# Building the new x from its normed form, and splitting the last ten expert matrices: one change to a decoder block with 32 experts

## The reference

```
h = rms_norm(x, g_mix);  z = h @ w_in + b_in          # w_in 1024 x 5376
y_conv = silu(layer_norm(conv31(glu))) @ w_conv_out + b    # 31 taps per channel
y_attn = window_attention(q, k, v, sinks) @ w_attn_out + b # window 128, 16 heads
x = x + (gate_conv * y_conv + gate_attn * y_attn) @ w_out
x = x + moe(rms_norm(x, g_ffn))     # 32 experts, top 4 per token, softmax weights
return rms_norm(x, g_final)
# one expert: a = (clip(u)+1) * g*sigmoid(1.702 g), g = min(x@w_gate+b, 7), u = x@w_up+b
#             y = a @ w_down + b     (each matrix 1024 x 1024, 4 MB)
```

## Time and profile before

| | us |
|---|---|
| runs shown: median (lowest, highest) of 3 | 1177.32 (1176.37, 1179.74) |
| the profiled execution | 1175.85 |
| its span in the profile | 1174.1 |
| TensorE busy in the span | 1120.3 |
| VectorE, ScalarE, GpSimd busy | 325.5, 179.7, 33.6 |
| mean DMA rate over the span | 376 GB/s |
| mean granted clock of TensorE | 0.999 |

### The profile page before, as it was taken

How to read it: one execution, slowest core, us unless ns; L and a number is a source line. 1 busy time by engine, 2 the same in 40 slices (tenths; PEclk the granted TensorE clock), 3 DMA queues, 4 the chain that set the end, 5 groups by cost and what they waited for, 6 DMA issues and landing times.

```text
span 1174.1 us, 13686 instructions
## 1 busy us (share of the span) xinstructions
PE 1120.3 (95%) x5333; PEld 530.4 (45%) x5333; DVE 325.5 (28%) x790; ACT 179.7 (15%) x351; POOL 33.6 (3%) x39
## 2 busy tenths in 40 slices
PE   7999999999999999999999999999999999999997
PEld 6888888854333333333333333333333333333332
DVE  1999973324111111121111111111111111111111
ACT  2111365222011001010011010000000000000011
POOL 2350000000000000000000000000000000000000
PEclk9999999999999999999999999999999999999999
DMA  8966435668999999999999999999999999999996
GB/s 270 349 209 187 143 117 207 251 269 308 408 428 428 433 431 430 429 433 432 433 430 432 430 434 433 431 431 431 430 437 432 431 430 431 434 432 432 431 424 258
DMA packets 54133, 441.69 MB, mean 376 GB/s; under 512 B 4183, under 2 KB 34137, under 8 KB 37336
## 3 DMA queue, kind: packets, MB, share of 16 engines
q1 hardware_dynamic: 53512, 440.20, 90.6%
q0 software_dynamic: 432, 0.95, 0.4%
q10 hardware_dynamic: 160, 0.13, 0.0%
HBM read 440.08 MB, written 1.05 MB: 376 GB/s over the span
## 4 chain that ended last, share of the span: by engine, by line
PE 90%; DMA 5%; another core or an unknown queue 2%; SPq 1%; issue 1%; DVE 0%; ACT 0%; ACTq 0%; DVEq 0%
PE bank L1426 54%; PE bank L1174 17%; PE bank L1394 5%; DMA arena<-in_w_up 4%; PE bank L1379 4%; PE bank L1290 2%; PE bank L1466 2%; PE bank L1436 1%; PE bank L1386 1%; PE bank L1473 1%; DMA arena<-in_g_ffn 1%; PE bank L1197 1%; PE bank L1223 0%; PE bank L1212 0%
## 5 line engine op out<-in xcount | busy, mean ns | idle before, releaser
L1426 PE MATMUL bank<-arena,x_columns 128*64 128x512 f32 x2080 | 468.2, 594 | 26.0 <-DMA arena<-in_w_up 24.5
L1426 PEld LDWEIGHTS bank<-arena,x_columns 128*64 128x64 f32 x2080 | 148.4, 137 | 299.9 <-issue 273.7
L1426 PE MATMUL bank<-arena,act_columns 128*64 128x512 f32 x992 | 219.1, 593 | 11.1 <-DMA arena<-in_w_down 11.1
L1174 PE MATMUL bank<-arena 128*128 128x256 f32 x928 | 205.3, 382 | 1.1 <-DVE arena L779 1.1
L1174 PEld LDWEIGHTS bank<-arena 128*128 128x128 f32 x928 | 176.5, 191 | 27.1 <-issue 1.7
L1426 PEld LDWEIGHTS bank<-arena,act_columns 128*64 128x64 f32 x992 | 76.1, 137 | 150.8 <-issue 150.8
L812 DVE SCALAR_TENSOR_TENSOR arena<-arena x240 | 96.4, 480 | 0.1
L1037 DVE TENSOR_SCALAR bias_selector<-ones_bf,expert_onehot 96x64 bf16<-96x64 bf16 x32 | 7.6, 237 | 270.9 <-PE bank L1386 270.9
L1071 DVE TENSOR_SCALAR gate_clipped<-bank 128x512 f32<-128x512 f32 x32 | 22.1, 692 | 202.8 <-PE bank L1426 202.8
L1075 DVE TENSOR_SCALAR hidden<-bank 128x512 f32<-128x512 f32 x32 | 22.1, 691 | 187.7 <-PE bank L1426 187.7
L1394 PE MATMUL bank<-y_block,scatter 64*128 64x512 f32 x248 | 61.5, 614 | 0.0
(11 more groups left out here) (190 smaller groups left out, 490.0 us busy)
## 6 DMA issues: line engine op xcount, KB each, us to landing
arena<-in_w_up SPq DMA_DIRECT2D x25, 4096.0 KB, 50.7
arena<-in_w_down SPq DMA_DIRECT2D x25, 4096.0 KB, 50.9
arena<-in_w_gate SPq DMA_DIRECT2D x24, 4096.0 KB, 49.9
arena<-in_w_in SPq DMA_DIRECT2D x21, 1024.0 KB, 11.8
arena<-in_w_gate SPq DMA_DIRECT2D x10, 2048.0 KB, 13.0
...
```

What stands on the lines that cost most here:

```text
L1174: last = pe.matmul(bank[n % 3][:, j * T:(j + 1) * T], w[:, c, j * P:(j + 1) * P], src[:, c, :], start=(c == 0), stop=(c == C - 1))
L1426: last = pe.matmul(dst[h * CAP:(h + 1) * CAP, :], lhs(row), cols(rows[:, row, :], h), start=(row == 0), stop=(row == MROWS - 1))
```

## The change

The new x is no longer put into Y with the identity ahead of the experts. It is rebuilt from `xh`: a diagonal matrix of the standard deviations (`scales`, two VectorE instructions behind `first_tokensT`) times `xh`, one of four halves in each of rounds 3 to 6. So Y now starts with the experts' down biases (`start_y`), x itself is dead once `xh` is written, and SyncE loads matrix 5's rows 6 and 7 on `xh_ready`. The small tiles of the softmax, the sinks and `before` now lie in the memory of `scales`. The expert weights are turned in bank 7 instead of bank 5, which takes a wait off the first up product. At the start, the vectors are loaded before conv_w, TensorE does half of piece 1 before it turns the vectors, and piece 2 before it turns the taps. Matrices 86 to 91 come in two transfers like 92 to 95 before, and one pass of the loop (two rounds) is written out. At the end, ScalarE's squares wait for single halves of Y, and VectorE's last steps have another order.

```diff
@@ -81,7 +81,8 @@
 
-WHOLES = range(3 * PAIRS, NM - 4)
+WHOLES = range(3 * PAIRS, NM - 10)
+LOOPS = range(LOOP0, (NM - 10) // PAIRS)
 ROW_PARTS = {n: [(0, 4), (4, 8)] for n in range(3)}
...
@@ -189,10 +190,13 @@
         ones_h = sb("ones_bf16", [P, P], bf16)
-        before = sb("strictly_before", [P, P], bf16)
+
+        scales = sb("x_scales", [P, TT, P])
+        before = scales[:, 0, 0:P // 2].bitcast(bf16)
+        sinks = scales[:, 1, 64:64 + NH]
+        early = scales[:, 1, 0:64].rearrange("p (k q n j) -> p k q n j", k=4, q=2, n=2)
         ndist = part(FREE0 + 4 * T + P, 2 * P)
         iota = sb("slot_iota", [P, 2, CAP])
-        sinks = sb("sinks", [P, NH])
         xT, actT = sb("x_columns", [P, 4, 2, CAP])[:], sb("act_columns", [P, 4, 2, CAP])[:]
...
@@ -381,11 +385,11 @@
                 if n == 1:
-                    sp.dma_start(cwrows, t_in["conv_w"]).then_inc(cw_loaded, 16)
                     for name, (row, rows) in VEC.items():
                         if name != "g_mix":
                             sp.dma_start(vrows[row:row + rows, :],
                                          t_in[name].rearrange("(c p) -> c p", p=P)).then_inc(vecs_loaded, 16)
+                    sp.dma_start(cwrows, t_in["conv_w"]).then_inc(cw_loaded, 16)
                     sp.dma_start(wrt, t_in["w_router"].rearrange("(c p) e -> p c e", p=P)).then_inc(wrt_loaded, 16)
...
@@ -432,22 +436,19 @@
             first_rows(4, 0, piece_done, WOUT0 + 3)
+            first_rows(5, 6, xh_ready, 1)
             first_rows(4, 2, piece_done, FRONT)
             first_rows(5, 3, piece_done, FRONT)
-            sp.wait_ge(xh_ready, 1)
-            first_rows(5, 6, x_added, 2)
+            first_rows(5, 7, xh_ready, TT)
             for n in range(PAIRS, WHOLES[0]):
-                for k, (lo, hi) in enumerate(parts_of(n)):
-                    if n == PAIRS and k == 3:
-                        sp.wait_ge(xh_ready, TT)
-                        first_rows(5, 7, x_added, 2 * TT)
+                for lo, hi in parts_of(n):
                     refill(n, lo, hi)
-            with sp.Fori(LOOP0, (WHOLES[-1] + 1) // PAIRS) as cycle:
+            with sp.Fori(LOOPS[0], LOOPS[-1] + 1) as cycle:
                 for i in range(PAIRS):
                     b, j = divmod(i + 1, 3)
                     sp.wait_ge(piece_done, cycle * (PAIRS * EW) + (FRONT + EW * (i - PAIRS) + EW))
                     load(i, 0, MROWS, rows_full[i, 0], cycle * ROUNDS + (b if j < 2 else b - 1), j)
-            for n in range((WHOLES[-1] + 1) // PAIRS * PAIRS, NM):
+            for n in range((LOOPS[-1] + 1) * PAIRS, NM):
                 for lo, hi in parts_of(n):
...
@@ -737,16 +738,26 @@
 
-            for t in range(TT):
-                act.wait_ge(y_done, t + 1)
-                for h in range(2):
-                    if (t, h) == (1, 1):
-                        act.wait_ge(gain_on, 1)
-                    act.activation((gmin, hidden)[h], Y[t][h][:], ACT.Square, accum_out=ss[:, 2 + h, t:t + 1]).then_inc(squares, 1)
+            def square(t, h):
+                act.wait_ge(y_done, 2 * t + h + 1)
+                if t == 1:
+                    act.wait_ge(squares, TT + h + 1)
+                act.activation((gmin, hidden)[h], Y[t][h][:], ACT.Square, accum_out=ss[:, 2 + h, t:t + 1]).then_inc(squares, 1)
+
+            def y_std(t):
                 act.wait_ge(squares_dve, t + 1)
                 act.activation(std[:, 0, t:t + 1], ss[:, 1, t:t + 1], ACT.Sqrt, scale=1.0 / D,
                                bias=eps[:, 0:1]).then_inc(stds, 1)
+
+            square(0, 0)
+            square(0, 1)
+            square(1, 0)
+            y_std(0)
+            act.wait_ge(gain_on, 2)
+            square(1, 1)
+            y_std(1)
             act.wait_ge(rstd_ready, TT)
+            act.wait_ge(gain_on, 2)
             act.activation(ysum[:, 1, 512:], ysum[:, 1, 512:], ACT.Copy, scale=rstd[:, 0, 1:2]).then_inc(last_half, 1)
...
@@ -1079,6 +1090,8 @@
             first_tokensT()
+            for t in range(TT):
+                dv.tensor_scalar(scales[:, t, :], ident[:], std[:, 1, t:t + 1], None, ALU.mult).then_inc(scales_ready, 1)
             dv.tensor_tensor(le, logits[:, :, 0:NE], m8[:, :, 0:1].to_broadcast([P, TT, NE]), ALU.subtract).then_inc(le_ready, 1)
...
@@ -1119,21 +1132,28 @@
 
+            def gained(t, h):
+                cols = slice(h * 512, (h + 1) * 512)
+                dv.tensor_tensor(ysum[:, t, cols], Y[t][h][:], gfin[:, cols], ALU.mult).then_inc(gain_on, 1)
+
             def half_out(t, h):
                 dv.wait_ge(rstd_ready, t + 1)
                 cols = slice(h * 512, (h + 1) * 512)
                 dv.scalar_tensor_tensor(ysum[:, t, cols], Y[t][h][:], rstd[:, 0, t:t + 1], gfin[:, cols],
                                         ALU.mult, ALU.mult).then_inc(ysum_ready, 1)
 
-            dv.wait_ge(y_done, 1)
+            dv.wait_ge(gfin_loaded, 16)
+            dv.wait_ge(squares, TT + 1)
+            gained(0, 0)
             sum_of_squares(0)
-            dv.wait_ge(gfin_loaded, 16)
-            dv.wait_ge(y_done, 2)
-            dv.tensor_tensor(ysum[:, 1, 512:], Y[1][1][:], gfin[:, 512:], ALU.mult).then_inc(gain_on, 1)
+            dv.wait_ge(y_done, 2 * TT)
+            gained(1, 1)
             y_rstd(0)
-            half_out(0, 0)
+            dv.wait_ge(rstd_ready, 1)
+            dv.wait_ge(gain_on, 1)
+            dv.tensor_scalar(ysum[:, 0, 0:512], ysum[:, 0, 0:512], rstd[:, 0, 0:1], None, ALU.mult).then_inc(ysum_ready, 1)
+            half_out(0, 1)
             sum_of_squares(1)
-            half_out(0, 1)
             y_rstd(1)
...
@@ -1231,16 +1251,18 @@
             project(0, hT, ready=hT_ready, ready_by=1)
+            project(1, hT, (0,))
             pe.wait_ge(vecs_loaded, 16 * (len(VEC) - 1))
             pe.wait_ge(vecs_out, 1)
             pe.transpose(bank[6][:, 0:VROWS], vrows, ident[0:VROWS, 0:VROWS]).then_inc(vecsT, 1)
-            project(1, hT)
+            project(1, hT, (1,))
+            project(2, hT)
             pe.wait_ge(cw_loaded, 16)
             for c in range(C):
                 last = pe.transpose(bank[7][:, c * KTAPS:(c + 1) * KTAPS], cwrows[:, c * P:(c + 1) * P],
                                     ident[0:KTAPS, 0:KTAPS])
             last.then_inc(cwT, 1)
-            for n in range(2, GATE0 + 1):
+            for n in range(3, GATE0 + 1):
                 project(n, hT)
...
@@ -1318,7 +1340,8 @@
 
-                pe.matmul(Y[t][h][:], ident[:], x[:, t, h * 512:(h + 1) * 512], start=True, stop=False).then_inc(x_added, 1)
+                pe.wait_ge(scales_ready, t + 1)
+                pe.matmul(Y[t][h][:], scales[:, t, :], by_eights(xh[:, t, :])[:, h * CAP:(h + 1) * CAP, :], start=False, stop=False)
 
...
@@ -1327,13 +1350,13 @@
                     pe.matmul(RANKS[1], ones_h[:], member_h[:, 0, :], start=True, stop=False)
-                pe.matmul(RANKS[t], before[:], member_h[:, t, :], start=(t == 0), stop=True).then_inc(rank_done, 1)
-
-            def first_gather(t):
+                pe.matmul(RANKS[t], before, member_h[:, t, :], start=(t == 0), stop=True).then_inc(rank_done, 1)
+
+            def first_gather(t, columns=range(C)):
 
                 pe.wait_ge(xh_ready, t + 1)
                 pe.wait_ge(sel_ready, t + 1)
-                for c in range(C):
+                for c in columns:
                     last = pe.matmul(FIRST_COLUMNS[t][c], xh[:, t, c * P:(c + 1) * P], sel[:, t, :], start=True, stop=True)
...
@@ -1365,10 +1388,9 @@
             sum_of_parts(1)
-            add_x(0, 0)
-            first_gather(0)
+            first_gather(0, range(5))
             ranks(1)
-            add_x(0, 1)
+            first_gather(0, range(5, C))
             first_gather(1)
...
@@ -1392,8 +1414,8 @@
                         last = pe.matmul(Y[t][h][:], sw[rows, t, :], y[rows, :], start=False, stop=ends)
-                    if ends:
-                        last.then_inc(y_done, 1)
+                        if ends:
+                            last.then_inc(y_done, 1)
 
...
@@ -1428,9 +1450,6 @@
                     last.then_inc(piece_done, 1)
-                    if i == 0:
-                        for h in between:
-                            add_x(1, h)
                     if i == 0 and bias is not None:
...
@@ -1443,14 +1462,13 @@
                         pe.matmul(Y[t][h][:], wT[:, t * P:(t + 1) * P], bdown[:, h * 512:(h + 1) * 512],
-                                  start=False, stop=False)
+                                  start=True, stop=False)
 
             def gate_product(b, n, cycle=None):
 
                 if n > 0:
                     pe.wait_ge(xT_ready, b + C)
-                product(A, n, lambda c: xT[:, c % 4, c // 4, :], bgate, cycle, ready=xT_ready if n == 0 else None,
-                        between=(0, 1) if n == 0 else ())
+                product(A, n, lambda c: xT[:, c % 4, c // 4, :], bgate, cycle, ready=xT_ready if n == 0 else None)
 
...
```

(14 more changed lines are left out.)

32 lines of the change are left out of this document (16 added, 16 removed).

## The result

The changed kernel took 1179.74 us (median of 20 runs, 1177.75 to 1185.4), the kernel before 1177.19 (20 runs on the same chip). The ratio is 1.0032, with a 95% interval of 1.0022 to 1.0042: slower, by 3.8 us. The medians alone are 2.6 us apart and the means 3.5, since five of the changed kernel's executions stand at 1184.2 us and above. The profiled executions are 3.9 us apart: a span of 1178.0 us against 1174.1. The forecast was 1181.0.

A forecast was written before the change was run, and what follows sets the result against it. Bound: when the DMA stream becomes continuous, bytes at 432 GB/s, and the tail. Terms 4.7 + 1.8 - 2.9 + 0.8 + 0.3 = +4.7 us gave 1180.6 or 1182.0 by base; forecast 1181.0, range 1177.0 to 1184.5.

The forecast's parts named there:

- likeliest case: Whole kernel: the forecast of 1181.0 us, own range 1178.8 to 1183.5, chance 0.60 together with D.
- Part 1: Start: TensorE's 1.3 us wait goes, but late taps make it wait 6.0 us at the sums: +4.7 us.
- Part 2: Behind the wait at the sums: TensorE's clock falls and restarts slowly, +1.8 us, bounds 0 and 3.6.
- Part 3: Router to first experts: without x matmuls TensorE leads by up to 3.7 us and loads go earlier: -2.9 us.
- rival A: Front and first experts: clock holds or recovers at once, stream recovers the full 3.7 us: +2.1 us; chance 0.24.
- D: Halves bring no gain, new x frees no room (-1.3, not -2.9): +6.3 us; chance inside the forecast's 0.60.
- Part 4: Last ten matrices: loading in halves gains 0 and lowers the transfer rate: +0.8 us, bounds 0 and 0.8.
- Part 5: Tail: ScalarE's squares start earlier, but the second token tile's sum queues on VectorE: +0.3 us, bounds -0.4 and +0.5.
- Rival C: Front: the convolution does not bind, so TensorE keeps its 1.3 us: -3.1 us, 1172.7 to 1174.2; chance 0.10.
- B: Front and first experts: slow clock restart in full and poor catching up: +8.3 us, 1184 to 1185.6; chance 0.06.

The follow-up runs named there:

- early taps: The changed kernel with conv_w's eight transpositions behind projection 1 again, not projection 2: 1174.75 us, ratio 0.9971 to the kernel before.
- the start alone: The kernel before with only the changed kernel's new order at the start: 1181.79 us, ratio 1.0046 to the kernel before.
- 8 calls: The changed kernel with 8 added matmul calls in TensorE's wait at the sums, their result overwritten: 1181.2 us, ratio 1.0035 to the kernel before.
- whole matrices: The changed kernel with matrices 86 to 91 loaded whole again: 1178.04 us, ratio 1.002 to the kernel before.
- x alone: The kernel before with only the new x and new end, keeping its start order and transfer sizes: 1175.51 us, ratio 0.9982.

## Why the forecast was right

Its interval and its likeliest case hold, and the main mechanism (VectorE's late taps, TensorE's wait at the sums, the slow clock behind it) is the one that the runs show. That the number is as near as it is is in part luck: the clock cost 0.6 us more than its term and the catch-up gave 1.0 more, and these pull opposite ways. Point by point:

- **Part 1, the wait.** Right (4.7 said, 4.53 measured): the copy at 33.72 us (33.97 said), the sums ready at 145.20 (145.4). The early taps and the start alone show it from both sides. Both profiles have the slow start, so it cancels.
- **Part 2, the clock.** The mechanism was right, the size short: +2.43 us (1.8), and up to 2.9 in other profiles. The nearest row, the start's projection, was slow in part only, while behind L1251 sums, scores and the projection all ran slow. The 8 calls show the cause: TensorE's rest, and not the scores waiting for VectorE. By the Trainium skill, "TensorE: Matmul & The Clock Gate", Part 1, rest throttles and activity releases; the fall at the sums agrees.
- **Part 3, the catch-up.** Leads of 1.24, 3.28 and 3.87 us (1.3, 3.2, 3.7 said) were right; the step that failed is the one that let the stream take back only 2.9 of them. It took all 3.87 (4.0 by the rates up to 337 us). That this is the x-part's is shown by the start alone, which gives nothing back, and by whole matrices, which keep the 56.24 us; no profile shows x alone with the clock held. The 2.9 came from serving the transfers one after the other from their issue times, which no row gives, so it can't be worked out again from the rows; the rates show room for more (299, 386 and 420 GB/s). In this one point rival A was right and D wrong.
- **Part 3, what wasn't in it.** I counted the x matmuls that left the router as pure gain. They were also what kept TensorE's clock up there. That has no term in the sum. It is seldom seen in the changed kernel: 5 of its 20 executions took 1184.2 to 1185.4 with a clock of 0.988 to 0.990. That these are the router's fall is argued, since none was profiled; with the clock kept at the sums, the taps early or x alone, one profiled execution of each has it, and the mean clock says that most others do.
- **Part 4, the halves.** +0.62 us (0.8 said), in two pairs of profiles. The gain is 0, as said: TensorE's waits for w_up in all went from 24.5 to 19.2 us and those for w_down stayed (11.1, 10.8), and the last wait is that of matrix 94 in both. By the Trainium skill, "DMA: Bandwidth & Descriptors", transfers of at least 1 MiB are asked for, and halves of 2 MB fulfil that; the runs show that they still have a small price, these 0.62 us.
- **Part 5, the tail.** From TensorE's end to the span's it is 7.05 us in both: 0, not +0.3. The second tile's sum did come 0.26 us later relative to TensorE's end (at 2.50 us, 2.24 before). But before, the reciprocal behind it on VectorE also had to wait for an output half of 0.75 us, and now that half stands ahead of the sum; so the last output half comes at 3.21 us where it came at 3.16. The prediction counted the new queue and not the one that it replaced.
- **Sum.** 4.53 + 2.43 - 3.87 + 0.62 + 0 = +3.7; 0.2 more stand between round 1 and the last wait, unexplained. Against the forecast's +4.7 the catch-up makes -1.0, the tail -0.3, the wait and the halves -0.2 each, the clock +0.6. Rival C was refuted by the wait itself, and B by the catch-up. The x matmuls moved into rounds 3 to 6 were hidden: from 684 to 755 us TensorE is busy for 71.00 of 71 us, where before it was for 66.32, so it meets the stream later and the end doesn't move by it.
